# A 512-column matmul for the high weight part in the first MLP product of a split-float32 kernel

## The reference

```
def _sq_relu_mlp(h, w1, w2):
    return jnp.square(jax.nn.relu(h @ w1)) @ w2

xl = _layer_norm(ALPHA * xl + g2_l * _sq_relu_mlp(xl * (1 + sc2_l) + sh2_l, w_ff1, w_ff2), ln2_g, ln2_b)
```

## Time and profile before

| | us |
|---|---|
| median of 3 runs | 2214.65 |
| lowest and highest | 2214.16, 2216.38 |
| profiled execution: its span, first to last instruction | 2212.9 |
| busy PE, DVE, ACT, POOL in the span | 2024.2, 1293.9, 812.6, 412.9 |
| first MLP matmul to last, by the windows | 1433 to 2179.4 |

### The profile page before, as it was taken

How to read it: one execution, slowest core, us unless ns; L and a number is a source line. 1 busy time by engine, 2 the same in 40 slices (tenths; PEclk the granted TensorE clock), 3 DMA queues, 4 the chain that set the end, 5 groups by cost and what they waited for, 6 DMA issues and landing times.

```text
span 2212.9 us, 38829 instructions
## 1 busy us (share of the span) xinstructions
PE 2024.2 (91%) x15438; PEld 1951.6 (88%) x15438; DVE 1293.9 (58%) x1270; ACT 812.6 (37%) x715; POOL 412.9 (19%) x320
## 2 busy tenths in 40 slices
PE   5889999998797888899998879899999999999996
PEld 4568999997787878789988879799999999999996
DVE  5784457676757666667667854554444544445445
ACT  5632224353444444433333223443333333333332
POOL 0000000004626312053011210025014204303500
PEclk9989999998999999999999989999999999999998
DMA  9934344444232344445666554335455554555540
GB/s 404 363 144 190 153 191 186 164 181 174 84 128 95 115 181 152 186 174 227 229 223 272 209 202 169 121 133 190 174 187 183 177 190 174 186 183 177 190 171 38
DMA packets 57156, 402.24 MB, mean 182 GB/s; under 512 B 6128, under 2 KB 8304, under 8 KB 9200
## 3 DMA queue, kind: packets, MB, share of 16 engines
q1 hardware_dynamic: 53568, 390.09, 47.6%
q10 hardware_dynamic: 3504, 10.99, 1.3%
HBM read 398.96 MB, written 2.10 MB: 181 GB/s over the span
## 4 chain that ended last, share of the span: by engine, by line
PE 66%; DVE 14%; ACT 6%; DMA 6%; DVEq 3%; issue 3%; POOL 2%; ACTq 0%; POOLq 0%; SPq 0%
PE main L1174 18%; PE main L1175 18%; PE main L1176 18%; DVE wlo L808 5%; ACT whi L395 4%; DVE asum L825 4%; DMA raw<-in_w_ada 2%; DVEq L824 2%; DMA raw<-in_w_in 2%; PE main L1259 1%; PE main L1260 1%; PE main L1261 1%; PE side L1450 1%; PE main L1194 1%; PE main L1195 1%
## 5 line engine op out<-in xcount | busy, mean ns | idle before, releaser
L808 DVE TENSOR_TENSOR wlo<-raw,whi 128x2048 fp32r<-128x2048 f32 x308 | 719.4, 2337 | 707.8 <-ACT whi L395 707.1
L395 ACT CAST whi<-raw 128x2048 fp32r<-128x2048 f32 x308 | 585.8, 1903 | 1056.8 <-PE main L1176 829.4
L1174 PE MATMUL main<-hL,whi 128*128 128x256 f32 x1568 | 460.3, 294 | 34.3 <-DVE wlo L808 22.0
L1175 PE MATMUL main<-hL,whi 128*128 128x256 f32 x1568 | 451.0, 288 | 0.0
L1176 PE MATMUL main<-hL,wlo 128*128 128x256 f32 x1568 | 450.4, 287 | 0.0
L1174 PEld LDWEIGHTS main<-hL,whi 128*128 128x128 f32 x1568 | 308.9, 197 | 40.4 <-DVE wlo L808 24.7
L1175 PEld LDWEIGHTS main<-hL,whi 128*128 128x128 f32 x1568 | 308.9, 197 | 1.7 <-issue 1.5
L1176 PEld LDWEIGHTS main<-hL,wlo 128*128 128x128 f32 x1568 | 308.4, 197 | 0.0
L1174 PE MATMUL main<-h,whi 128*128 128x256 f32 x1024 | 292.5, 286 | 9.4 <-DVE h L1101 5.8
L1175 PE MATMUL main<-h,whi 128*128 128x256 f32 x1024 | 292.1, 285 | 0.0
L1176 PE MATMUL main<-h,wlo 128*128 128x256 f32 x1024 | 292.0, 285 | 0.0
(11 more groups left out here) (238 smaller groups left out, 3153.7 us busy)
## 6 DMA issues: line engine op xcount, KB each, us to landing
raw<-in_w_f SPq DMA_DIRECT2D x128, 1024.0 KB, 4.8
raw<-in_w_in SPq DMA_DIRECT2D x108, 1024.0 KB, 6.4
raw<-in_w_ada SPq DMA_DIRECT2D x96, 1024.0 KB, 6.1
raw<-in_w_br SPq DMA_DIRECT2D x24, 1024.0 KB, 5.8
raw<-in_w_out SPq DMA_DIRECT2D x16, 1024.0 KB, 4.9
xin<-in_xT ACTq DMA_DIRECT2D x1, 4096.0 KB, 23.6
ax<-in_xT ACTq DMA_DIRECT2D x1, 2048.0 KB, 8.8
out<-acc ACTq DMA_DIRECT2D x4, 512.0 KB, 2.7
```

What stands on the lines that cost most here:

```text
L395: nc.scalar.copy(split_place(name, s)[0], raw[:, slot]).then_inc(hi_made, 1)
L808: TT(lo, raw[:, slot], hi.bitcast(F32), ALU.subtract).then_inc(lo_made, 1)
L1174: mm(out, w_hi, x_hi, start=start, stop=False, skip_group_check=skip)
L1175: mm(out, w_hi, x_lo, start=False, stop=False, skip_group_check=skip)
```

## The change

In the first MLP product the high weight part meets the high and the low activations in one matmul of 512 columns. The bank's first half then holds w_hi x_hi + w_lo x_hi and its second half w_hi x_lo. ACT copies the first half of each bank to `h4`, DVE adds the second half to it into `sqb` and frees the bank, and POOL takes the relu ahead of the square, with a further drain, into rows 4 to 7 of `sqb`. In the last row tile the low weights come first, so that the matmul over the whole bank is the last. The second product and all other stages keep `three`.

```
+            def halves_out(f, i):
+                for b in range(4):
+                    blk("mlp", f * 8 + i, 0, b)
+                    nc.scalar.copy(h4[:, b], main[:, b, 0:T]).then_inc(half_out, 1)
             def mlp(f, last):
                 if isinstance(f, int) and f == 0:
                     for k in (2, 3):
                         split("mlp", 0, k + 1)
+                    halves_out(0, 0)
                 with act.Fori(1 if isinstance(f, int) and f == 0 else 0, 4) as i:
                     for k in range(4):
                         split("mlp", f * 8 + i, k + 1)
+                    halves_out(f, i)
...
                         wait(pool, freed["V"], f * 32 + i * 4 + (PH["mlp"].f0["V"] + b + 1))
-                        TT(sqb[:, b], sqb[:, b], sqb[:, b], ALU.mult)
+                        nc.gpsimd.tensor_scalar_max(sqb[:, 4 + b], sqb[:, b], 0.0)
+                        drain()
+                        TT(sqb[:, b], sqb[:, b], sqb[:, 4 + b], ALU.mult)
                         drain()
                         two_parts([hid[:, i * 4 + b, n] for n in range(2)], sqb[:, b], hid_lo)
...
                         blk("mlp", f * 8 + i, 0, b)
-                        nc.vector.tensor_scalar_max(sqb[:, b], main[:, b, 0:T], 0.0).then_inc(freed["V"], 1)
+                        wait(dve, half_out, f * 16 + i * 4 + (b + 1))
+                        TT(sqb[:, b], h4[:, b], main[:, b, T:], ALU.add).then_inc(freed["V"], 1)
...
+            def two(out, w_hi, w_lo, x_both, x_hi, start, stop):
+                if not stop:
+                    mm(out, w_hi, x_both, start=start, stop=False)
+                last = mm(out[:, 0:T], w_lo, x_hi, start=False, stop=False, skip_group_check=True)
+                if stop:
+                    last = mm(out, w_hi, x_both, start=False, stop=True)
+                return last
...
+                            elif both:
+                                last = two(main[:, b], w_hi, w_lo, x[:, kt].rearrange("p v t -> p (v t)"), x[:, kt, 0],
+                                           start, stop)
...
-                    panel("mlp", f * 8 + i, 0, 0, h2, ready=lambda k: pe.wait_ge(h2_lo, k + 1))
+                    panel("mlp", f * 8 + i, 0, 0, h2, ready=lambda k: pe.wait_ge(h2_lo, k + 1), both=True)
```

More of the change, by code:

```diff
@@ L273, in build @@
          pool_y, m_done, m_lo, ax_in, mean_ps, mu_in, cen_done, sq_done, var_ps, rstd_in, h2_tmp, h2_hi,
-         h2_lo, acc_zero, hid_lo, passed, res_done, y_out, cleared) = (sem(x) for x in (
+         h2_lo, acc_zero, half_out, hid_lo, passed, res_done, y_out, cleared) = (sem(x) for x in (
             "cst_in x_in pool_ld ax_ld stored silu_sig silu_in silu_hi silu_lo mods_ps h_tmp h_hi h_lo "
@@ L279, in build @@
             "pool_y m_done m_lo ax_in mean_ps mu_in cen_done sq_done var_ps rstd_in h2_tmp h2_hi "
-            "h2_lo acc_zero hid_lo passed res_done y_out cleared").split())
+            "h2_lo acc_zero half_out hid_lo passed res_done y_out cleared").split())
         def wait(eng, semaphore, value):
@@ L1176, in three, with panel @@
                 return mm(out, w_lo, x_hi, start=False, stop=stop, skip_group_check=skip)
-            def panel(name, it, n, first, x, with_ctx=False, ready=None, between=lambda k: None):
+            def two(out, w_hi, w_lo, x_both, x_hi, start, stop):
[5 more added lines that the diff above has]
+                return last
+            def panel(name, it, n, first, x, with_ctx=False, ready=None, between=lambda k: None, both=False):
                 chunks = PH[name].panels[n][0]
```

## The result

The changed kernel takes 2236.35 us (median of 4 runs, 2233.82 to 2241.25) against 2214.40 for the kernel before: ratio 1.0101, interval 1.0084 to 1.0119. It is slower by 22 us; the forecast was 7.7 faster.

What follows compares the result with a forecast made beforehand. PE was taken to bound the kernel, without a hole in 31 of 32 MLP panels. The matmul saving of -12.9 us and POOL's waits of +5.2 us sum to -7.7: forecast 2206.9 us, range 2200.8 to 2211.0.

Steps and rivals of the forecast that it cites:

- Where PE is bound: MLP from its second panel on: PE busy for all of 714.30 us, so a change of its work is worth full size.
- what the exit costs: Way out of PSUM by ACT's copy and DVE's add, in the first product's panels: tight but covered, costed at nothing.
- cover of 0.66 us: Time between the end of DVE's split for the next panel's second chunk (4.88) and PE wanting it (5.55).
- The pair, -12.9 us: First MLP product: 512 plus 256 columns take 346.7 ns for 360, saving 13.3 ns a group, 12.9 us together.
- POOL's hole: Fourth chunk of the first panel on hid: PE waits 1.3 us for POOL, once in each of four turns, +5.2 us.
- the rule: POOL and a DVE split take turns in the order they came; it gave the old timeline E + 13.60, measured 13.62.
- the deadline: PE wants all hidden blocks of the turn's fourth panel at E + 17.28, E being that panel's end.
- I take 0.40, near the copy: Assumed duration in us of POOL's new relu, between 0.31 and 0.61, or 1.2 if it ran like two passes.
- The walk: POOL's four blocks followed from the fourth panel's end through three DVE splits: last subtract ends at E + 18.33.
- Block 0: start -0.50: POOL begins the fourth panel's first block 0.50 us before E, after DVE frees its bank at -0.68.
- A bit over 2 might: Clock behind POOL's idle: 1.3 us costs no clock, an idle a bit over 2 us might lower it.
- POOL much slower: Rival, chance 0.09: relu of 0.7 to 0.9 us gives 2216.4; from 0.95 a fourth split, 20.8 holes, 10.8 falls, 2233.

Runs made afterwards that it cites:

- pair_only: Changed kernel with only PE's matmul edit: no ACT copies, DVE takes the relu of the first half, POOL as before; 2205.35 us against 2211.94, ratio 0.9974.
- halves_of_256: Changed kernel with the relu on DVE after its add and three 256-column matmuls a group again; 2211.74 us, ratio 0.9997 to the kernel before.
- no_relu: Changed kernel without POOL's relu and its drain, the relu left out of the result; 2206.83 us, ratio 0.9976 to the kernel before.
- same_operand: Changed kernel with POOL's square taking the relu's output as both inputs; 2218.37 us, ratio 1.0021 to the kernel before.
- pool_relu_only: Kernel before with only POOL's relu and its drain added ahead of the square, DVE keeping its relu; 2224.73 us, ratio 1.0068.
- halves_pool: Changed kernel with its whole way out, but the first product made of three 256-column matmuls again; 2225.80 us, ratio 1.0062 to the kernel before.
- dve_relu: Changed kernel with the relu on DVE after its add, POOL as in the kernel before; 2205.07 us, ratio 0.9977; again 2208.65, ratio 0.9967.

## Why the prediction was wrong

- **Where PE is bound, and what the exit costs: right.** PE was without a hole before, and a change of its work is worth its size (pair_only, halves_of_256). The exit over ACT and DVE, costed at nothing, costs nothing while POOL is quick (no_relu). In the changed kernel POOL eats up its cover of 0.66 us: in the second and third turn the second split of the fourth panel ends some 0.03 us after PE wants it, and these two panels take 22.79 us in place of 22.6. The row in the second turn:

```profile
1704.84 0.19 PEld L1191 LDWEIGHTS main<-h,whi 128*128 128x128 f32 x1 [0.25 <-DVE wlo L817]
```

- **The pair, -12.9 us: the term was mis-sized.** It measured -6.6. "No row shows the two sizes alternating" was the open point. The bounds held (gain 5 to 40 ns a group; it is 6.7), but I took the uniform rows.
- **POOL's hole: the place, the rule and the deadline were right, the length was not.** This is the step that failed. I took +5.2 us in four holes of 1.3; the holes are 21.4 and the chunks behind them lose 8.8 more. Two things are in the 21.4, and the third came on top:
  - The durations. "I take 0.40, near the copy" failed: the relu is 0.85 with 0.15 behind it, twice the 0.40 and the estimate of 0.38 beside it. The copy moves data and has no scalar, and no row bore out that a relu costs the same. And the square slowed from 0.61 to 0.74, since it no longer reads one tile twice (same_operand has it at 0.61 again). The subtract of two different tiles with its 0.75 stood in the earlier trace rows beside the square, and I did not ask why they differed. Together 0.50 us a block. The walk with these numbers ends at E + 19.7: a hole of 2.4 us. That is what the first panel of the second, third and fourth turn shows, and pool_relu_only and halves_pool in full.
  - The walk covered one panel from a clean start. "Block 0: start -0.50" is not true in the fourth panel: POOL's end at 19.7 holds up the split that DVE issues at 19.2, and the next panel starts 0.34 later. It then meets a fourth split, ends at 22.1 and hands its delay on in turn. In the fourth panel, the one that PE waits for, POOL starts at 0.0 and the hole is 5.2. Same_operand and halves_pool each take one condition away, POOL's half us and the shorter panel, and the slide is gone.
  - The clock. "A bit over 2 might" was right: it fell behind all four holes of 5 us, and behind six of the eight with some 2.2 of idle (pool_relu_only, halves_pool). It cost 8.8 us, a term that the sum did not have, since its hole was 1.3.
- **The rival that came true** is "POOL much slower", with a fourth split, holes of 20.8 and falls of 10.8, at a chance of 0.09. Its condition was wrong, though. I had put the fourth split at a relu of 0.95 us. A relu of 0.85 with a square of 0.61 does not reach it (same_operand); with the square at 0.74 it does, because the panels hand their delay on. So the closeness of its 2233 is in part luck.

With the measured pair, the holes and the falls (-6.5 + 21.4 + 8.8 + 0.2) the sum is +23.9 us, 2238.5 on the median of before, 2 us above the measured one.

## What to carry to other kernels

Work moved to an engine "with time in hand" has to be walked through for several periods, with each thing that takes turns with it: here one period gives a hole of 2.4 us, and the hand-over of the delay from one to the next makes it 5.2. A duration for an operation that the trace does not show should be bounded by rows with as many distinct operands and the same kind of operand, and where such a bound spans a threshold, the chance belongs on both sides of it. Matmuls of two widths are better run in long groups of one width: here groups of sixteen left 1.0 of the 6.7 ns.

## What the runs showed of the hardware

- POOL: a relu with a scalar on 128 x 256 float32 takes 0.845 us; a product of two tiles 0.74, of one tile with itself 0.61 (same_operand). The same relu on DVE takes 0.29 to 0.57 (dve_relu).
- POOL beside DVE's split (2.29 us, two inputs in SBUF): a POOL instruction of 0.6 to 0.85 us that is issued inside a split takes 2.4 to 2.9 us, and a split issued inside a POOL instruction up to 2.88.
- PE: float32r matmuls of 256 columns start 120.0 ns apart, of 512 columns 226.7, each in a uniform run; a pair of them in turn takes 353.3.
- The granted clock stayed at 1.00 behind three of four idles of 1.91 to 1.93 us, and behind two of eight of 2.15 to 2.27; behind the others the next 5.9 us had a mean of 0.71 to 0.74. The length of the idle alone does not tell: two idles of 2.15 in pool_relu_only went either way, and so did the 2.82 us in the last layer norm. With fillers that cut the idle to 0.24 to 1.28 us it stayed at 1.00 all four times.
